# The end of the recurrent mixer: output products inside the chunk chain, bonus on other banks, mean taken out of V, one operation per state

## The reference, cut to what matters

```python
def step(state, inp):                                   # per token, per head, state 64x64
    r_t, w_t, k_t, v_t, kk_t, a_t = inp
    sa = jnp.einsum('bhvk,bhk->bhv', state, -kk_t)
    state = (state * w_t[:, :, None, :]
             + sa[..., None] * (kk_t * a_t)[:, :, None, :]
             + v_t[..., None] * k_t[:, :, None, :])
    return state, jnp.einsum('bhvk,bhk->bhv', state, r_t)
_, y = lax.scan(step, state0, xs)
mu = jnp.mean(y, axis=-1, keepdims=True)                # over the 64 of a head
var = jnp.mean(jnp.square(y - mu), axis=-1, keepdims=True)
y = (y - mu) * lax.rsqrt(var + RWKV_GN_EPS)
y = y * ln_g + ln_b
y = y + jnp.sum(rh * kh * r_k, axis=-1, keepdims=True) * vh      # the bonus
y = y.reshape(B_, S_, A_WIDTH) * g
...
yb = mla_attention(zb, ...)                             # 6 heads, softmax, then rms_norm
yc = gmlp_spatial_gate(zc, ...)
x = x + jnp.concatenate([ya, yb, yc], axis=-1) @ w_out[l]
```

## Time and profile before

| | us |
|---|---|
| median of 3 runs | 3194.45 (3190.31 to 3198.06) |
| the profiled execution: its time | 3195.96 |
| the profiled execution: its span in the trace | 3194.2 |
| PE busy in the span | 3016.3 (94%) |
| DVE busy | 2332.0 (73%) |
| ACT busy | 1742.3 (55%) |
| mean granted TensorE clock | 0.963 |

### The profile page before, as it was taken

The page is one execution under the profiler, slowest core; times in us unless marked ns, Lnnn a source line. Parts: engine busy times, 40 slices in busy tenths (PEclk is TensorE's granted clock), DMA queues, the critical chain, the costliest instruction groups (busy, mean ns, idle before and its releaser), DMA issues. The chain is left out here.

```text
span 3194.2 us, 52514 instructions
## 1 busy us (share of the span) xinstructions
PE 3016.3 (94%) x18304; PEld 2494.1 (78%) x18305; DVE 2332.0 (73%) x3614; ACT 1742.3 (55%) x2220; POOL 50.5 (2%) x57
## 2 busy tenths in 40 slices
PE   7999898999999999988789988799999999999999
PEld 3687546998888999977659976678888888888887
DVE  3665763889788666666545465588998998998998
ACT  3444303335533444446224363278888888888886
POOL 0000000000000000000000000000000000000000
PEclk9999899999999999989889998889999999999999
DMA  7561152455677666641135331199999999999995
GB/s 278 212 222 64 39 205 69 149 162 185 254 252 230 217 204 211 208 148 66 54 146 182 113 125 37 69 381 412 388 383 363 379 383 361 382 379 364 391 368 219
DMA packets 228409, 738.94 MB, mean 231 GB/s; under 512 B 23783, under 2 KB 60056, under 8 KB 225432
## 3 DMA queue, kind: packets, MB, share of 16 engines
q1 hardware_dynamic: 222936, 704.95, 59.9%
q0 software_dynamic: 4160, 27.79, 2.9%
q10 hardware_dynamic: 1152, 4.19, 0.3%
HBM read 707.48 MB, written 29.36 MB: 231 GB/s over the span
## 5 line engine op out<-in xcount | busy, mean ns | idle before, releaser
L3837 DVE TENSOR_TENSOR moe_lo<-moe_raw,moe_hi 128x1024 fp32r<-128x1024 f32 x756 | 887.3, 1220 | 66.5 <-ACT moe_hi L3664 46.1
L3664 ACT ACTIVATE moe_hi<-moe_raw 128x1024 fp32r<-128x1024 f32 x756 | 791.1, 1061 | 154.9 <-PE moe_pB L3597 87.4
L3597 PE MATMUL moe_pB<-moe_hi,moe_hEh 128*128 128x512 f32 x1008 | 399.1, 396 | 0.3 <-DVE moe_hEl L3902 0.3
L3597 PE MATMUL moe_pB<-moe_hi,moe_hEl 128*128 128x512 f32 x1008 | 393.1, 390 | 0.0
L3597 PE MATMUL moe_pB<-moe_lo,moe_hEh 128*128 128x512 f32 x1008 | 392.7, 390 | 0.0
L3597 PEld LDWEIGHTS moe_pB<-moe_hi,moe_hEl 128*128 128x128 f32 x1008 | 189.2, 188 | 40.8
L3597 PEld LDWEIGHTS moe_pB<-moe_hi,moe_hEh 128*128 128x128 f32 x1008 | 189.4, 188 | 39.2 <-issue 1.7
L3597 PEld LDWEIGHTS moe_pB<-moe_lo,moe_hEh 128*128 128x128 f32 x1008 | 189.5, 188 | 37.6
L3615 PE MATMUL moe_pB<-moe_hi,moe_ah 128*128 128x512 f32 x504 | 197.0, 391 | 5.6 <-DVE moe_al L3846 5.6
L1941 PE MATMUL exp_pO<-exp_vh,exp_ah 128*128 128x512 f32 x512 | 200.1, 391 | 1.6 <-DVE exp_al L2026 1.6
L1941 PE MATMUL exp_pO<-exp_vl,exp_ah 128*128 128x512 f32 x512 | 200.0, 391 | 0.0
(11 more groups left out here) (815 smaller groups left out, 6706.3 us busy)
## 6 DMA issues: line engine op xcount, KB each, us to landing
moe_raw<-in_moe_w SPq DMA_DIRECT2D x758, 512.0 KB, 6.9
value_ring<-in_peer_v SPq DMA_DIRECT2D x128, 512.0 KB, 4.3
...
```

Source lines behind the costliest of these rows:

```text
L3597: i = pe.matmul(pB[:, kind], l[:, kd], m[:, n % HALVES, ns], start=kd == 0 and x == 0, stop=kd == KD - 1 and x == 2)
L3664: act.activation(hi[:, n % HALVES], raw[:, n % RING], ACT.Copy).then_inc(hi_ready, 1)
L3837: dve.tensor_tensor(lo[:, n % HALVES], raw[:, n % RING], hi[:, n % HALVES], ALU.subtract).then_inc(lo_ready, 1)
```

## The change

- PE: the transposes of `o` move from between `X` and `Z` into the last chunk's step. The y products move into the chain: in each step RK·V and RT·S stand behind the product with the state and ahead of the wait for Z, and RB·Z behind the increment of the state. The bonus' sums move from behind the first pair's y into the first chunk's step, onto the attention's banks `M`.
- DVE: the copy of `Q` comes ahead of `o`. The next state is one instruction for all three pairs: the decayed old state is multiplied out earlier into a new tile `decayed`, and one addition from PSUM makes the state. The bonus times v stands in chunk 1's step, the scaling of `o` in chunk 2's, the addition of `ln_b` behind the chain.
- ACT: the copies of `X` come ahead of the squares of `o`, those of `Z` ahead of the root.
- V is multiplied by a new mask `centre` (identity less 1/64) in place of the identity, so that y has no mean. The steps that took the mean off are gone; ACT squares y straight from PSUM, and DVE divides straight from PSUM; the copy of y to SBUF is gone. The constant tile of masks grows from 10 to 11.

```diff
-                fill("V", "VT", None)
+                fill("V", "VT", "centre")
...
                 fill("X", "At", "TT", f"T{LEVELS - 1}", "AT")
-                pe.wait_ge(q["m_on_ready"], 1)
-                for a in range(TT):
-                    for j in range(3):
-                        i = pe.transpose(M[a][:, j * P:(j + 1) * P], o[:, a, j * P:(j + 1) * P], k.ident[:])
-                i.then_inc(q["m_ot_psum"], 1)
                 fill("Z", "TT", "W", "Q")
+
+                def y_part(lhs, rhs, p, ck, start=False, stop=False):
+                    x = p * NCH + ck
+                    for s in HALVES:
+                        i = pe.matmul(pB[p][s, ck * CH:(ck + 1) * CH], bd[lhs][s, x], S[s, p, ck] if rhs == "S" else bd[rhs][s, x], start=start, stop=stop)
+                    return i
...
                         i.then_inc(q["u_psum"], 1)
-                        pe.wait_ge(q["u_read"], c)
...
+                            y_part("RK", "V", p, ck, start=True)
+                            y_part("RT", "S", p, ck)
+                        if ck == NCH - 1:
+                            pe.wait_ge(q["m_on_ready"], 1)
+                            pe.wait_ge(q["bonus_read"], 1)
...                              (the transposes of o)
+                        pe.wait_ge(q["u_read"], ck)
...                              (the state's increment, then:)
+                    if ck == 0:
+                        for p in range(AT):
+                            y_part("RK", "V", p, ck, start=True)
+                    for p in range(AT):
+                        i = y_part("RB", "NT", p, ck, stop=True)
+                        if ck == NCH - 1:
+                            i.then_inc(q["y_psum"], 1)
+                    if ck == 0:
                         pe.wait_ge(q["bonus_in"], 1)
+                        pe.wait_ge(q["m_s_ready"], BHEADS)
+                        pe.wait_ge(q["m_pt_read"], BHEADS)
...                              (the bonus' sums, to BONUS on banks M)
                 for p in range(AT):
                     act.wait_ge(q["y_psum"], p + 1)
-                    act.activation(ys[:, p * NCH:(p + 1) * NCH, :], pB[p][:, 0:T].rearrange("p (c n) -> p c n", n=HD), ACT.Copy).then_inc(q["ys_ready"], 1)
+                    act.activation(L[:, p], pB[p][:, 0:T], ACT.Square).then_inc(q["ysq_ready"], 1)
...
                         dve.wait_ge(q["s_psum"], ck + 1)
-                        for p in range(AT):
...
-                                i = dve.scalar_tensor_tensor(out=S[:, p, ck + 1], in0=S[:, p, ck], scalar=Wend[:, p * NCH + ck:p * NCH + ck + 1],
-                                                             in1=src, op0=ALU.mult, op1=ALU.add)
+                        src = pA[1][:, 0:AT * CH].rearrange("p (j n) -> p j n", n=CH)
...
+                            c.settle()
+                            dve.tensor_tensor(S[:, :, ck + 1], src, decayed[:], ALU.add).then_inc(q["s_read"], 1)
+                        if ck < NCH - 2:
+                            dve.wait_ge(q["s_read"], ck + 1)
+                            c.tick(dve.tensor_tensor(decayed[:], S[:, :, ck + 1], by_chunk(Wend[:])[:, :, ck + 1].unsqueeze(2).to_broadcast([P, AT, CH]), ALU.mult))
...
-                def centre(p):
+                def spread(p):
                     m = slice(p * NCH, (p + 1) * NCH)
-                    dve.wait_ge(q["ys_ready"], p + 1)
-                    c.link(dve.tensor_reduce(st1[:, m], ys[:, m], AX_X, ALU.add))
-                    c.link(dve.tensor_scalar(st1[:, m], st1[:, m], 1.0 / HD, None, ALU.mult))
-                    c.link(dve.tensor_tensor(ys[:, m], ys[:, m], wide(st1[:, m]), ALU.subtract))
-                    sqy = L[:, p].rearrange("p (c n) -> p c n", n=HD)
-                    c.link(dve.tensor_tensor(sqy, ys[:, m], ys[:, m], ALU.mult))
-                    c.link(dve.tensor_reduce(st2[:, m], sqy, AX_X, ALU.add))
+                    dve.wait_ge(q["ysq_ready"], p + 1)
+                    c.link(dve.tensor_reduce(st2[:, m], L[:, p].rearrange("p (c n) -> p c n", n=HD), AX_X, ALU.add))
                     dve.tensor_scalar(st2[:, m], st2[:, m], 1.0 / HD, GN_EPS, ALU.mult, ALU.add).then_inc(q["mean_ready"], 1)
```

More of the change, by code:

```diff
@@ L3051, in _ @@
                         dve.tensor_tensor(Z, pA[0][:, 0:AT * CH].rearrange("p (j n) -> p j n", n=CH), Z, ALU.add).then_inc(q["u_read"], 1)
+                    if ck == 1:
+                        dve.wait_ge(q["bonus_psum"], 1)
+                        for j in range(AT):
+                            i = c.tick(dve.tensor_tensor(kkb[:, j], BONUS[j], vx[:, j], ALU.mult))
+                        c.settle()
+                        dve.nop().then_inc(q["bonus_read"], 1)
+                    if ck == 2:
+                        dve.wait_ge(q["m_oroot_ready"], 1)
+                        c.link(dve.reciprocal(f1[:], f3[:]))
+                        for a in range(TT):
+                            i = dve.scalar_tensor_tensor(out=o[:, a], in0=o[:, a], scalar=f1[:, a:a + 1], in1=og[:], op0=ALU.mult, op1=ALU.mult)
+                        i.then_inc(q["m_on_ready"], 1)
```

96 lines of the change are left out of this document (40 added, 56 removed).

## The result

The changed kernel took 3171.02 us as the median of 4 runs (3163.74 to 3173.08), the kernel before, beside it on the same chip, 3193.56 (3190.31 to 3198.06). The ratio is 0.9924, with a 95% interval of 0.9903 to 0.9945: 0.76% faster, and 22.5 us instead of the 28 forecast. 3171 lies in the range of 3160 to 3179. In the profiled executions the span fell from 3194.2 to 3171.2, by 23.0 us.

A forecast was written before the change was run, and what follows sets the result against it. Bound at the mixer's end by a chain of short steps in which one engine waits for another. Layer 0 gains 3.4 + 7.2 + 2.9 = 13.5, layer 1 16.1, together 29.6, less 1.6: 28; forecast 3167 us, range 3160 to 3179.

The forecast's parts named there:

- The start of the chain: Before the chunk chain in layer 0: it starts at 1572.35 instead of 1575.72, 3.4 us gained.
- The clock: TensorE's clock in the new chain: expected at 2.4 GHz until the tail; a fall at the start loses 6.7 us a layer.
- The chain's steps: In the chunk chain: products with the state follow after 2.7, 2.65 and 2.8 us, y complete at 10.3 to 10.5.
- part 2: The chunk chain with the outputs y in layer 0: 10.5 us instead of 17.7, 7.2 gained.
- The tail: Behind y in layer 0, bound mostly by DVE: 7.1 us instead of 10.0, 2.9 gained.
- A: Clock falls in the new chain too, losing 6.7 us in one layer or 13.4 in both: 3173 to 3180; chance 0.18.
- B: Work in DVE's chain gaps binds more and ACT's copies collide with DVE, 2 to 3 us a layer: 3172; chance 0.12.
- C: Clock is high when the next stage starts, thanks to a shorter tail, 2 us a layer: 3163; chance 0.12.
- D: Gain spent elsewhere, for instance output products not overlapping in the chain; about 10 us left over both layers: 3185; chance 0.02.
- E: Clock stays at 1.2 GHz from the chain through the next stages' products, net 30 us slower: 3225; chance 0.02.
- faster: Whole kernel faster by more than 0.2%, 6.4 us: chance 0.96.
- The sum: Both layers' stretches: 13.5 and 16.1 us, together 29.6, less 1.6 for nops, settles and table loads: 28.

The follow-up runs named there:

- f2: Kernel before with only the earlier chain start (copies of Q, X, Z first; scaling and transposes of `o` behind the chain); stretches 34.2 and 34.6 us.
- g3: Kernel before with idle matmuls added in PE's waits in the chain; y complete at 13.86 us in both layers, stretches 33.3 us.
- f3: Changed kernel with the y products and the bonus behind the chain again, pair by pair; stretches 27.3 and 27.9 us.
- g2: Changed kernel with the load of `w_out` issued only once y is complete; stretches 23.19 and 23.20 us, span 3168.5.
- g4: Changed kernel with the mean taken off by DVE again, from a copy of y; tail 11.77 us in both layers for 7.03.
- f1_again: Changed kernel again without an edit; 3170.63 us as the median of 6 runs, ratio 0.994 to the kernel before.
- k1: Changed kernel with second half of `w_out` loaded later, Z's copies ahead of the squares, transposes and copy to `oT` last; 3158.23 us, ratio 0.9891 to before.
- k2: Changed kernel with only the second half of the `w_out` load held back to the last increment of the state; 3166.45 us in one run.

## Why the prediction was right, and where it was not

- **The start of the chain** (3.4 us): right. Start 5.42 behind phase Q for 5.6, gained 3.6 in layer 0. (The prediction's terms, 1571.3 and 0.92, add up to 1572.2 and not 1572.35, which brings the forecast nearer still.) It is worth less alone (f2: 2.5); in layer 0 the clock fell sooner there.
- **The clock**, the unknown with the largest price: right in direction and place. Chains with PE's waits filled stayed at 2.4 GHz (six of eight of the changed kernel's, both of g3), chains with waits of 0.4 to 0.8 us in every step ran at 1.2 GHz for the most part (before, f2, f3). g3 shows it as a cause, with the same chain. The Trainium skill, "TensorE: Matmul & The Clock Gate", section "HAM oscillation — how this bites in real kernels", lays the low rate to long idle gaps between bursts. The traces here don't agree: f3's chain fell behind waits of 1.05, 0.46 and 0.46 us, and g3's, with its waits filled, kept 2.4 GHz.
- **The chain's steps** (2.7, 2.65, 2.8, then to 10.5): steps 1 and 2 measured 2.60 and 3.07, the first 3.36, y at 11.60 for 10.5: this term was 1.1 us too small in layer 0. Two causes. The first step without a pause is 3.03 (g2): 0.74 for the increment, 0.80 for the 24 records of y, and 1.49 for the bonus that I had at 1.3. And PE's pauses, 0.33 and 0.62 us in layer 0 of this profile, 0.47 and 0.82 in layer 1, up to 1.10 in the changed kernel's others. The forecast did not have them at all: it looked at the load of `w_out` only for whether it is done in time. With the load moved away the stretch is 23.2, the forecast's number; but there 0.2 too much in the steps stands against a start 0.2 earlier.
- **The split of part 2**: 7.2 were forecast and 6.1 came, but putting the outputs and the bonus into the chain is worth only 3.2 and 3.5 us net (f3): the tail behind them is 1.9 longer, 1.0 of it since pairs that come one after the other hide a part of the tail.
- **The tail**: 7.03 for 7.1, and the arithmetic that went is worth 4.7 a layer (g4) for 4.65. With the arithmetic left in, the tail would have grown from 10.0 to 11.8 (g4).
- **Rivals.** A came in two of eight stretches, at 1.6 us (f1_again, y) of the 6.7 priced. B, no: where PE doesn't pause the two steps that hold DVE's added work took 2.59 and 2.55 us (g2) for the 2.65 and 2.8 priced. C, no: the clock is 0.67 in 1590 to 1595 and 0.50 in 1595 to 1600, and both distances behind the stretches stayed within 0.4 us. D and E, no. (The chance of "faster" should read 0.97 by the prediction's own terms, not 0.96.)
- **The sum**: 29.6 less 1.6 was 28; the stretches gave 27.5 against the profile it was made from, 25.9 against the second profile of before. There layer 1's stretch was 37.6 and not 39.3, so 1.7 of the 28 rested on one profile of layer 1, with its chain start at 10.86 for 8.98. The medians of three comparisons give 22.5, 17.8 and 23.6. The gap of the profiled pair is not in the mixer: phase Q of layer 0 starts at 1566.7 and 1563.4 in the kernel before, at 1570.6, 1571.0, 1572.2 and 1565.8 in the changed one, and at 1561.4 to 1568.8 in the variants of it. The mask that the change adds is loaded far behind the stage in which the difference arises (k1 and k2 above), which scatters by 6 us with the place of its low clock. That profiles scatter this way is shown. That scatter also explains the medians' 18 to 24 us for 25.9 to 27.5 of the stretches is not: all three comparisons fall short, and the stage from 297 us on was longer in all four profiles of the changed kernel than in those of before. A cost of some microseconds that the changed program brings to a stage it doesn't touch is an open rival. The range held the result, the middle did not allow for it.
